# Residual rows in DRAM during the expert stage, and a third down-weight buffer, in a two-layer streaming encoder

## What is computed

```python
x = x + mixer(rms_norm(x, norm_mix[layer]))
xn = rms_norm(x, norm_ffn[layer])
# hier_moe: the best of 4 groups, in it the best 2 of 8 experts, gates from softmaxes
hid = silu(xn @ w_gate[e]) * (xn @ w_up[e])      # 1024 -> 256, for each of 32 experts
x = x + sum_k gate[k] * (hid_k @ w_down[e_k])    # 256 -> 1024
# after two layers: y = rms_norm(x, norm_final)
```

## Time and profile before

| | |
|---|---|
| median of 3 runs | 1278.65 us |
| profiled execution: time | 1279.65 us |
| profiled execution: span from first to last instruction | 1278.0 us |
| TensorE (matmul) busy | 1063.3 us, 83% |
| VectorE (DVE) busy | 493.3 us, 39% |
| ScalarE (ACT) busy | 289.6 us, 23% |
| GpSimd (POOL) busy | 272.5 us, 21% |
| DMA moved | 303.67 MB, mean 238 GB/s |
| chain that ended last | PE 58%, DMA 21%, DVE 10%, issue 8%, ACT 2% |

### The profile page before, as it was taken

The page is one execution under the profiler, slowest core; times in us unless marked ns, Lnnn a source line. Parts: engine busy times, 40 slices in busy tenths (PEclk is TensorE's granted clock), DMA queues, the critical chain, the costliest instruction groups (busy, mean ns, idle before and its releaser), DMA issues.

```text
span 1278.0 us, 14398 instructions
## 1 busy us (share of the span) xinstructions
PE 1063.3 (83%) x5242; PEld 609.9 (48%) x5242; DVE 493.3 (39%) x1066; ACT 289.6 (23%) x616; POOL 272.5 (21%) x289
## 2 busy tenths in 40 slices
PE   6999999998995978887854999987985978788870
PEld 5777777774543333332323777743543323333320
DVE  3234444344356111110116699993455111111116
ACT  3233232333111101000003455553111100000002
POOL 3000000000003111111042488850003111101033
PEclk9999999999995999988885999998996989999895
DMA  8953322302706999999955922100027999999963
GB/s 278 389 172 109 109 97 78 106 22 105 296 36 227 408 419 420 420 420 421 414 174 132 367 61 66 33 25 0 34 101 286 413 421 421 421 420 420 379 255 131
DMA packets 107791, 303.67 MB, mean 238 GB/s; under 512 B 18248, under 2 KB 65480, under 8 KB 82745
## 3 DMA queue, kind: packets, MB, share of 16 engines
q1 hardware_dynamic: 85481, 254.74, 51.4%
q0 software_dynamic: 22256, 48.22, 10.4%
HBM read 278.34 MB, written 57.12 MB: 262 GB/s over the span
## 4 chain that ended last, share of the span: by engine, by line
PE 58%; DMA 21%; DVE 10%; issue 8%; ACT 2%; SPq 1%; POOL 0%; DVEq 0%; POOLq 0%
DMA ring<-in_w_up 16%; PE bank L1200 12%; PE bank L522 10%; PE bank L421 7%; PE bank L1217 6%; PE bank L549 4%; DVE bank L1680 2%; PE bank L1478 2%; PE bank L572 2%; PE bank L1190 2%; PE bank L588 2%; PE bank L613 2%; PE bank L346 2%; DMA work<-in_w_pw 1%; PE bank L954 1%
## 5 line engine op out<-in xcount | busy, mean ns | idle before, releaser
L1200 PE MATMUL bank<-ring,work 128*64 128x512 f32 x704 | 179.1, 667 | 34.9 <-DMA ring<-in_w_up 33.1
L1217 PE MATMUL bank<-ring,work 128*64 128x512 f32 x528 | 124.9, 616 | 36.7 <-DVE work L1236 22.4
L1478 PE MATMUL bank<-arena,work 128*128 128x288 f32 x512 | 129.2, 415 | 8.2 <-issue 3.2
L1200 PEld LDWEIGHTS bank<-ring,work 128*64 128x64 f32 x704 | 61.4, 153 | 150.3 <-issue 147.8
L522 PE MATMUL bank<-arena,ring 128*128 128x288 f32 x512 | 131.9, 412 | 0.0
L1232 DVE TENSOR_TENSOR work<-work,bank 128x256 f32<-128x256 f32 x33 | 13.9, 421 | 292.2 <-ACT work L1228 292.2
L1478 PEld LDWEIGHTS bank<-arena,work 128*128 128x128 f32 x512 | 99.0, 195 | 38.0 <-issue 8.3
L1627 POOL TENSOR_TENSOR ring<-ring 128x606 f32<-128x606 f32 x76 | 103.8, 1365 | 55.8 <-ACT ring L1576 46.2
L522 PEld LDWEIGHTS bank<-arena,ring 128*128 128x128 f32 x512 | 94.9, 190 | 32.6 <-issue 7.9
L421 PE MATMUL bank<-ring,arena 128*128 128x512 f32 x224 | 100.9, 604 | 6.6 <-ACT arena L1611 6.6
L1680 DVE SCALAR_TENSOR_TENSOR bank<-work,ring,bank 128x606 f32<-128x606 f32 x129 | 98.8, 844 | 0.0
(11 more groups left out here) (256 smaller groups left out, 1293.9 us busy)
## 6 DMA issues: line engine op xcount, KB each, us to landing
ring<-in_w_down SPq DMA_DIRECT2D x32, 2048.0 KB, 24.1
ring<-in_w_gate SPq DMA_DIRECT2D x22, 2048.0 KB, 22.0
ring<-in_w_up SPq DMA_DIRECT2D x22, 2048.0 KB, 28.9
arena<-in_w_gate SPq DMA_DIRECT2D x10, 2048.0 KB, 23.0
arena<-in_w_up SPq DMA_DIRECT2D x10, 2048.0 KB, 31.1
ring<-in_w_qkv SPq DMA_DIRECT2D x24, 512.0 KB, 6.0
y_sorted<-gain POOLq DMA_DIRECT2D x8, 1536.0 KB, 5.7
work<-in_w_pw SPq DMA_DIRECT2D x16, 512.0 KB, 5.1
```

The source lines that it names most:

```text
L1200: mm = nc.tensor.matmul(bank[2 + s][rr, :], xte[s][:, c, rr], wgu[g][:, :, e, c, :], start=c == 0, stop=c == C - 1)
L1217: mm = nc.tensor.matmul(bank[5 + h][rr, :], hts[:, c, rr], wdn[s][:, e, c, h * HALF:(h + 1) * HALF], start=c == 0, stop=c == FC - 1)
L1478: mm = nc.tensor.matmul(bank[banks[h][w]][:, 0:GT], wp[s][:, w, c, :], xt[:, c, h * GT:(h + 1) * GT], start=c == 0, stop=c == C - 1)
```

## The change

x becomes the first of three spaces of the arena (x, xn, xt), and gain gets a third row. The third gate/up slot now lies in the first 4096 columns of x (gate half) and of xn (up half). There is a third down slot: for the first expert of a pair the last 1024 columns of x and of xn, for the second the first two rows of gain. Extra pairs get a slot of their own, in xn, xt and a part of the ring. As x is overwritten, each tile of it is stored to x_keep in DRAM right behind the x_rows store of that tile, and read back when pair 14 has done its down matmuls; the combine waits for it. The norm weights of the next layer are loaded behind that, since gain[:, 0] is part of the third down slot. Neither half of block 2 waits for far rows any more. They are in first_loads with dn 2. All ten early gathers are made, and all ten late ones are small; the table slot and its copy on DVE are gone. All far-row scatters now stand between pairs 0 to 9. Two small DVE tiles share space with a third.

```diff
-        x = sb("x", [P, TILES, D])
-        arena = sb("arena", [P, 2 * TILES * D])
+        arena = sb("arena", [P, 3 * TILES * D])
+        x = arena[:, 0:TILES * D].rearrange("p (j d) -> p j d", j=TILES)
...
-        gain = sb("gain", [P, 2, D])
+        gain = sb("gain", [P, 3, D])
...
+        def two_spaces(n):
+            spaces = arena[:, n * TILES * D:(n + 2) * TILES * D].rearrange("p (w r) -> p w r", w=2)
+            return spaces[:, :, 0:2 * C * FE], spaces[:, :, 2 * C * FE:2 * C * FE + D]
+        EXTRA = GU_SLOTS
+        gu_spaces, dn_spaces = zip(two_spaces(0), two_spaces(1))
...
-            do(V.tensor_copy(slot[:], slot_f[:]))
...
-            for n in range(FAR_FIRST):
-                far_rows(*far[n])
...
-                if local < 2 * TILES - FAR_FIRST:
-                    far_rows(*far[FAR_FIRST + local])
+                if local < 2 * TILES:
+                    far_rows(*far[local])
...
-                            if early(j, k):
-                                y_rows_in(pool, j, k, early_slot)
+                            y_rows_in(pool, j, k, early_slot)
...
-                    y_rows_in(pool, j, k, late_slot if early(j, k) else slot)
+                    y_rows_in(pool, j, k, late_slot)
...
+            dve.wait_ge(x_in[j], 16 * (2 * l + 3))
...
+        def dn_slot(l, local):
+            g = local % DN_SLOTS
+            per_layer = len(range(g, EPAIRS, DN_SLOTS))
+            return g, 16 * (1 if g < 2 else 2) * (per_layer * l + local // DN_SLOTS + 1)
...
+            for n in range(2):
+                sp.dma_start(wdn[s][n], src[:, n, :, :]).then_inc(base.dn_in[s], 16)
...
                     sp.dma_start(x_rows[j * P:j * P + rows[j], :], xf[0:rows[j], j, :]).then_inc(x_out, 16)
+                    sp.dma_start(x_keep[j * P:j * P + rows[j], :], x[0:rows[j], j, :]).then_inc(x_in[j], 16)
...
                 gu_load(sp, l, 1, (1,))
+                if l == 1:
+                    sp.wait_ge(proj_ev, 2 * TILES * (l + 1))
+                    dn_load(sp, l, 1)
+                gu_load(sp, l, 2, (1,))
+                for j in range(TILES):
+                    sp.wait_ge(x_in[j], 16 * (2 * l + 2))
                 gu_load(sp, l, 2, (0,))
+                dn_load(sp, l, 2)
...
-                down_first = local >= GU_SLOTS
-                if local + GU_SLOTS < EPAIRS and not down_first:
-                    sp.wait_ge(base.gu_mm, i + 1)
-                    gu_load(sp, l, local + GU_SLOTS)
-                if local + 2 < EPAIRS:
-                    sp.wait_ge(base.dn_mm, i + 1)
-                    dn_load(sp, l, local + 2, local % 2)
-                if local + GU_SLOTS < EPAIRS and down_first:
-                    gu_load(sp, l, local + GU_SLOTS)
+                sp.wait_ge(base.gu_mm, i + 1)
+                gu_load(sp, l, local + GU_SLOTS)
+                sp.wait_ge(base.dn_mm, i + 1)
+                dn_load(sp, l, local + DN_SLOTS)
...
-            sp.wait_ge(x_out, 16 * TILES * (l + 1))
-            sp.wait_ge(far_first, 16 * FAR_FIRST * (l + 1))
-            gu_load(sp, l, 2, (1,))
-            sp.dma_start(gain[:, 0, :], broadcast(norm_mix[l + 1] if l + 1 < LAYERS else norm_final)).then_inc(gain_in, 16)
...
-            for local in range(EPAIRS):
+            for local in range(EPAIRS - GU_SLOTS):
                 loads(local)
             sp.wait_ge(base.dn_mm, EPAIRS * (l + 1) - 1)
             with sp.If(count > 0):
                 extra_loads(0)
+            for j in range(TILES):
+                sp.dma_start(x[0:rows[j], j, :], x_keep[j * P:j * P + rows[j], :]).then_inc(x_in[j], 16)
+            sp.dma_start(gain[:, 0, :], broadcast(norm_mix[l + 1] if l + 1 < LAYERS else norm_final)).then_inc(gain_in, 16)
```

More of the change, by code:

```diff
@@ L139, in encoder @@
         shift = sb("shift", [P, EXPERTS])
-        place = sb("place", [P, 2, TILES, EXPERTS])
-        at_slot = sb("at_slot", [P, 2, TILES, EXPERTS])
+        slot_sets = sb("slot_sets", [P, 2 * 2 * TILES * EXPERTS])
+        place, at_slot = (slot_sets[:, n * 2 * TILES * EXPERTS:(n + 1) * 2 * TILES * EXPERTS].rearrange(
+            "p (k j e) -> p k j e", k=2, j=TILES) for n in range(2))
+        ocmp = slot_sets[:, 0:OVER * EXPERTS].rearrange("p (o e) -> p o e", o=OVER)
         slot_f = sb("slot_f", [P, 2, TILES])
         orow = sb("orow", [P, OVER])
-        ocmp = sb("ocmp", [P, OVER, EXPERTS])
         oexp = sb("oexp", [P, OVER])
@@ L213, in encoder @@
         ot = xn_flat[:, 0:C * TOKENS].rearrange("p (c t) -> p c t", c=C)
[L216 to L218 removed]
+        def two_spaces(n):
[3 more added lines that the diff above has]
+        gu_spaces, dn_spaces = zip(two_spaces(0), two_spaces(1))
+        wgu = [ring[:, s, 0:4 * C * FE].rearrange("p (w e c f) -> p w e c f", w=2, e=2, c=C) for s in range(2)] + [
+            a.rearrange("p w (e c f) -> p w e c f", e=2, c=C) for a in gu_spaces]
+        wdn = [[ring[:, s, (4 + n) * C * FE:(5 + n) * C * FE].rearrange("p (c n) -> p c n", c=FC) for n in range(2)]
+               for s in range(2)] + [[dn_spaces[0], gain[:, 0:2, :]],
+                                     [dn_spaces[1], ring[:, 1, 2 * TILES * D:(2 * TILES + 2) * D].rearrange("p (c n) -> p c n", c=FC)]]
         part = cut(work[:], [D, D, D, D, FE, FE, FE, D])
@@ L224, in encoder @@
         hid_pc = hid.rearrange("p (q c) -> p c q", c=FC)
-        ysb = [part[7], gain[:, 1, :]]
+        ysb = [part[7], gain[:, 2, :]]
         part = cut(work[:], [2 * C * P, 2 * C * P, SPAN, SPAN, TOKENS])
@@ L250, in encoder @@
         b2 = rest[:, acc_at:acc_at + D]
-        raw = gain[:, 1, :]
+        raw = gain[:, 2, :]
         DIAGS = P * (LAST_PE - 8)
@@ L289, in __init__ @@
                 self.y_free = sem(f"{tag}_y_free") if slots == 1 else None
-                self.x_in, self.dn_in, self.y_out = two("x_in"), two("dn_in"), two("y_out")
+                self.x_in, self.y_out = two("x_in"), two("y_out")
+                self.dn_in = [sem(f"{tag}_dn_in{s}") for s in range(slots if slots == 1 else DN_SLOTS)]
                 self.gu_in = [sem(f"{tag}_gu_in{s}") for s in range(slots if slots == 1 else GU_SLOTS)]
@@ L1150, in experts_pool, with landed @@
                         for k in range(2):
-                            if early(j, k):
-                                y_rows_in(pool, j, k, early_slot)
-        def early(j, k):
-            return k == 0 or j < EARLY_TILES
-        def landed(j, layers, late=True):
-            each = [1 + (late and early(j, k)) if late else early(j, k) for k in range(2)]
-            before = [1 + early(j, k) for k in range(2)]
-            return 16 * (sum(before) * (layers - 1) + sum(each))
+                            y_rows_in(pool, j, k, early_slot)
+        def landed(layers, late=True):
+            return 16 * (4 * (layers - 1) + 2 * (1 + late))
         def y_rows_in(pool, j, k, part):
@@ L1202, in ex_up_pe, with ex_down_pe @@
             mm.then_inc(m.gu_mm, 1)
-        def ex_down_pe(pe, m, i, s, k, loads):
+        def ex_down_pe(pe, m, i, s, g, there):
             pe.wait_ge(m.hid, i + 1 + FREE)
@@ L1209, in ex_down_pe @@
             pe.wait_ge(m.ht_ev, i + 1)
-            pe.wait_ge(m.dn_in[s], 16 * loads * (k + 1))
+            pe.wait_ge(m.dn_in[g if m is base else 0], there)
             pe.wait_ge(m.y_ev_a, i + FREE)
@@ L1439, in conv_first @@
         def conv_first(sp):
-            sp.wait_ge(gathered[0], landed(0, 1))
+            sp.wait_ge(gathered[0], landed(1))
             conv_load(sp, 0, 0)
@@ L1789, in _ @@
             steps.done(pool.memset(mean_w[:], 1.0 / D))
-            steps.done(pool.memset(gain[:, 1, :], 0.0))
+            steps.done(pool.memset(gain[:, 2, :], 0.0))
             for s in range(2):
```

66 lines of the change are left out of this document (31 added, 35 removed).

## The result

The changed kernel is slower by 0.7%, twice what a measurement can tell from no change: 1288.08 us (median of 6 runs, 1287.22 to 1292.08) against 1279.65 (median of 6 runs of the kernel before, 1277.28 to 1281.58), a ratio of 1.0067 with a 95% interval of 1.0051 to 1.0082. The forecast was 1273.0, and its range (1266.5 to 1282) does not hold the result.

The account below looks back on a forecast made before the run. The prediction took the expert stages' weight stream, at 421 GB/s, to bound the kernel. Its terms, -3.2 - 4.2 + 2.5 + 0 - 0.8 = -5.7 us, against 1278.65 gave 1273.0 us, range 1266.5 to 1282.

Parts of the forecast that it names:

- What bounds the kernel: Both expert stages: each ends when its weight stream resumes plus the remaining bytes divided by 421 GB/s.
- Parts 1 and 2: Stage start: 4.72 MB less behind the hole, later resumption, pair 0 late; stages end 3.2 and 4.2 us earlier.
- part 3: Stage end: x reload delays last scatter 2.5 us (0 to 4.9) in layer 0, 0 (to 2.3) in layer 1.
- rival B: Stage start: first gather must see the prefetch backlog out; +7.3 us, 1286; chance 0.15, shared with other slowdowns.
- Part 4: After the stage: late gathers of tiles 3 and 4 become small; gain 0.8 us in layer 0, 0 in layer 1.
- Nothing: Items priced at zero: removed DVE copy, far-row scatters between pairs, third down buffer's deeper queue, unchanged block order.
- rival A: The hole moves: first gather 10.9 us in both layers, layer 0's last scatter 8.2; +1.5 us, 1280.2; chance 0.28.

Follow-up runs that it names:

- e1: Changed kernel with the reload of x and the gain row issued only behind the last scatter: 1282.86 us, ratio 1.0017 to the kernel before.
- e5: Changed kernel with the gain row alone issued at the very end of the stage: 1286.0 us, ratio 1.0051 to the kernel before.
- e6: Changed kernel with the reload of x alone issued at the very end of the stage: 1284.35 us, ratio 1.0034 to the kernel before.
- e7: Changed kernel with both the reload of x and the gain row at the very end of the stage: 1286.66 us, ratio 1.0035 to the kernel before.
- e11: Kernel before plus only the round trip of x (stored to DRAM, reloaded after pair 14's down matmuls): 1290.28 us, ratio 1.0081.
- e2: Changed kernel with eight early gathers as before, late ones of tiles 3 and 4 full again: 1281.63 us, ratio 1.0012 to the kernel before.
- e13: Kernel before with unused gather rows fetching token 0 instead of being skipped, 3.7 MB more per layer: 1284.52 us.
- e9: Changed kernel with four tiles of x reloaded earlier, when pair 14's gate/up matmuls are done: 1291.95 us, ratio 1.0096 to the kernel before.
- e15: Changed kernel; block 2/dn 2 prefetch held for first gather, x tile 0 reloaded at stage end, rest after tile 0's late gathers, eight early gathers: 1279.37 us, 0.9987.
- e14: Changed kernel; block 2/dn 2 prefetch held for first gather, x tile 0 reloaded at stage end, rest after tile 0's late gathers, ten early gathers: 1281.54 us, 1.0014.

## Why the prediction was wrong, step by step

**What bounds the kernel:** right. The stage runs at 419 GB/s, and its end moved with the resumption and the bytes behind it.

**Parts 1 and 2:** right in mechanism and size. The first gather was to take 8.5 us and took 8.52 and 8.24; pair 0 was to be 4.2 and 1.5 us late and is 4.4 (412.33, from 407.95) and 1.3 (988.67 - 977.51 against 980.65 - 970.75); block 3 was forecast at about 422 and was issued at 421.82. The stages were to end 3.2 and 4.2 us earlier, and did so by 3.5 and 5.8; over the five executions with the same stages (after, e1, e5, e6, e7) the means are 3.2 and 5.0. One thing of part 3 hides in the 3.5: the scatter waited 1.1 us for POOL. The prediction had the ten gathers "ending just as pair 15 is evicted", with 0.2 us to spare by the times of before. The gathers start behind pair 14's scatter and so moved with the stage, but from that scatter to the end of pair 15's eviction there were now 12.25 us in place of 13.19, and the ten gathers need 12.65. By the rule that an engine takes turns between its rows (the Trainium skill, "DMA: Bandwidth & Descriptors", "Queues, rings and completion order") a gather beside a backlog does not have to see it out; the trace agrees: it landed at 409.4, in the middle of a window that moved 373 GB/s, and rival B's mechanism did not occur, though its 1286 comes near the result.

**Part 3, the reload:** this step failed. "+2.5, the middle" of 0 to +4.9 for layer 0, and 0 with a bound of +2.3 for layer 1; measured, S0-L0 +10.3, and S1-X +7.0. Both are outside their bounds. By e11, e2 and e5 the +10.3 is 6.9 for the round trip of x, 2.4 for the two gathers and 0.9 for the gain row, with the reserve made at e11; the +7.0 is 2.0, 3.4 and 1.6.

The step had three faults. First, it took 0.73 and 0.49 of free engine time as room for 8.5 us of traffic. That share is a mean over 16 engines; e13 and the packet counts show them unequally loaded a few microseconds earlier, and from 665 to 670 of the changed kernel, while the scatter is waited for, one to three packets are under way at most moments. An average of free time says nothing of the engine on which the last piece of the scatter lies.

Second, the upper bound was a row in which the scatter meets other traffic of one kind (8.2 us); here reload, gain row and ten gathers are all issued ahead of it, and the row was no bound. The reload's pieces landed 6.8 to 14.7 us after their issue in layer 0 and 17.9 to 25.8 in layer 1.

Third, moving the bytes was not priced as a whole. 2.36 MB had to pass between pair 14 and the combine, and in this stretch transfers are waited for in turn: the last scatter, the extra pair's weights, the late gathers, and in layer 0 the next layer's first rows and weights. e1, e6, e7, e9 and e15 put the reload in front of, between and behind them, and found a bill in the next piece of the ledger (e7: S0-L0 back at 5.0, X-end 37.3; e9: S1-X 22.9; e15: X-end 37.2). Its size depends on the place. The pieces outside the stages (S0-L0 with L0-G1, and S1-X with X-end) are longer than before by 10.1 and 6.7 us in the changed kernel, by 6.0 and 5.1 in e15, by 3.1 and 5.5 in e14, and by 0.9 and 6.9 in e7 (an execution below its median). e15, the fastest kernel, so pays back about what the filled hole brings.

A DMA counts as done when the last of its up to 16 engines is (the Trainium skill, "DMA: Bandwidth & Descriptors", "Why a DMA increments its semaphore by 16 and not by 1"). The trace agrees with it: in layer 0 the scatter landed at 671.4, after a stretch of 5 us at 0.23 busy.

Bytes alone do not explain every window. From 1240 to 1250 of the changed kernel the engines are busy and yet slow:
```profile
1240.00:1245.00 5.00, 3.71 (x18) 1.57 (x18) 0.85 (x2) 0.08 (x1) 0.00 (x0) 1.00 1.04 309
1245.00:1250.00 5.00, 0.45 (x3) 0.00 (x0) 0.69 (x1) 0.58 (x1) 0.00 (x0) 1.00 0.96 244
```
The packet records show what is slow: a packet of 4 KB takes 0.25 us from 1245 to 1250, on both queues, where it took 0.16 from 1235 to 1240. Why stays open, but neither the gain row nor the reload is needed for it: in e5, without the gain row, it is 0.26 to 0.29 from 1240 to 1245, and in e7, with neither, 0.26 from 1231 to 1236. The records do not name the engine, so which engines the rows of an indirect DMA lie on is not shown; that they are unequal is inferred from e13's windows and the packet counts.

**Part 4:** the step held, its gain of 0.8 us did not show. The combine of tile 3 no longer waits for its gather, but all of it is 6.9 us later (693.98, from 687.12), tile 2 waits 4.1 us, and L0-G1 is 0.2 us shorter, not 0.8.

**"Nothing":** right for the stores of x. Neither half of block 2 or dn 2 came late; the window up to 405 is full.

**The rivals and the chances.** That the changed kernel could be slower had 0.15, and the one mechanism named for it was the first gather, the one wait that I had looked at from both ends. The reload was in the sum with a middle value; it had no rival of its own, and rival A took the last scatter only up to the same 8.2 us. The chain had shown that the last scatter and the late gathers stand in it: whatever is put ahead of them is paid at its landing, not at its mean.

## What to carry to other kernels

Before a buffer's contents are parked in DRAM to fill a hole at one end of a stage, find the place for the way back. If the other end is a chain of small DMAs that depend on each other, price the transfer by what it delays in that chain, and begin with its bytes by rate: here 2.36 MB are 5.6 us at 421 GB/s. Ahead of the last scatter they cost 6.9 us of S0-L0 in e11, and the fastest kernel, e15, still had 6.0 and 5.1 us more outside its stages. Look also at what stands behind the transfer in the issuing queue: in e15 that was the next layer's first loads. A free share in a window is a mean over engines and no room for a prefetch: look at how the stream before it runs out. When a list of an engine is "just in time" in the trace of before, a microsecond added to it, or taken from its cover, is on the path.

## What the runs showed of the hardware

The last scatter of layer 0, a tile of half-used rows, took 3.3 us when the last of eight gathers had been issued 4 us ahead of it, 5.5 to 5.7 directly behind ten gathers, 9.9 with eight gathers and a 2.36 MB reload ahead, and 13.3 with the gain row and two gathers more; in layer 1 that last case was 20.7. The last blocks of a weight stream that shares the engines with short indirect transfers landed at 82 GB/s, not at 421, with three packets under way in place of 16: 3.7 MB of added gathers made the last matmuls 1.5 us and the stages 2.3 to 2.7 us later, in one execution, where the rate would make it 9. Beside the gathers from y_sorted at the end of layer 1 a packet of 4 KB took 0.25 to 0.29 us (after, e5, e7), against 0.16 within the stage. A first gather beside a full backlog of 2 MiB loads took 8.2 to 8.5 us, against 4.3 alone, and did not wait for the backlog to end.
